# Stick-breaking attention on one core: half a group of weights times values moved to the head of its step

## What is computed

```
def sb_attend(q, q_pos, k, v, k_pos):
    z = jnp.einsum('bqhd,bkhd->bhqk', q, k, preferred_element_type=jnp.float32) * (SB_HEAD_DIM ** -0.5)
    mask = (k_pos[None, :] < q_pos[:, None])[None, None]
    log_keep = jnp.where(mask, jax.nn.log_sigmoid(-z), 0.0)
    suffix = lax.cumsum(log_keep, axis=3, reverse=True) - log_keep
    a = jnp.where(mask, jnp.exp(jax.nn.log_sigmoid(z) + suffix), 0.0)
    return jnp.einsum('bhqk,bkhd->bqhd', a.astype(v.dtype), v)
```

## Time and profile before

| | us |
|---|---|
| median of 3 runs | 2764.31 |
| lowest, highest | 2760.12, 2768.33 |
| the profiled execution | 2768.86 |
| its span, first to last instruction | 2765.2 |
| TensorE busy | 2667.1 (96%) |
| ScalarE busy | 1156.7 (42%) |
| VectorE busy | 1733.0 (63%) |
| GpSimd busy | 732.0 (26%) |

### The profile page before, as it was taken

One profiled execution on the slowest core, in us unless ns is written; L12 is line 12 of the kernel. 1 busy time (PEld: TensorE's weight loads), 2 busy tenths in 40 slices (PEclk: granted clock), 3 DMA queues, 4 the chain that ended last, 5 costly groups with the idle time before them and its releaser, 6 DMA issues. The chain is left out here.

```text
span 2765.2 us, 40402 instructions
## 1 busy us (share of the span) xinstructions
PE 2667.1 (96%) x14531; PEld 2236.8 (81%) x14531; DVE 1733.0 (63%) x2331; ACT 1156.7 (42%) x2260; POOL 732.0 (26%) x627
## 2 busy tenths in 40 slices
PE   7989998999999999999899999998999999999998
PEld 6878887788888878888798887776878888788886
DVE  5656666376555688888410008887485555788887
ACT  4334445343333333344322219998343333333433
POOL 3200001135544400000221116666045544300001
PEclk9999999999999999999999999999999999999999
DMA  4211122514444573533234437763324444654342
GB/s 150 86 61 46 46 79 89 184 60 153 137 137 144 170 256 125 162 122 118 80 128 151 155 102 194 172 173 121 111 95 145 137 137 145 235 181 164 127 154 100
DMA packets 285877, 368.81 MB, mean 133 GB/s; under 512 B 25984, under 2 KB 205696, under 8 KB 285696
## 3 DMA queue, kind: packets, MB, share of 16 engines
q1 hardware_dynamic: 285696, 366.42, 41.7%
HBM read 242.19 MB, written 124.16 MB: 132 GB/s over the span
## 5 line engine op out<-in xcount | busy, mean ns | idle before, releaser
L2342 DVE TENSOR_TENSOR x<-m_ps,x 128x1024 f32<-128x1024 f32 x224 | 273.3, 1220 | 91.9 <-PE m_ps L79 91.8
L2051 POOL TENSOR_TENSOR m_u<-m_u,m_u 128x512 f32<-128x512 f32 x128 | 179.6, 1414 | 349.0 <-DVE m_u L2185 344.0
L1998 POOL TENSOR_SCALAR m_stat<-m_stat 128x1 f32<-128x1 f32 x36 | 12.1, 335 | 831.6 <-ACT m_sqjunk L1942 667.2
L2173 DVE TENSOR_TENSOR m_z<-m_ps,m_part 128x512 f32<-128x512 f32 x96 | 66.3, 691 | 143.8 <-PE m_ps L79 143.5
L1800 ACT COPY m_part<-m_ps 128x512 f32<-128x512 f32 x96 | 56.4, 588 | 205.2 <-PE m_ps L79 205.2
L2161 DVE TENSOR_TENSOR m_up<-m_upr,m_up 128x512 fp32r<-128x512 f32 x128 | 87.9, 707 | 28.5 <-ACT m_up L1787 28.5
L3300 ACT ACTIVATE e_b<-e_ps 128x512 f32<-128x512 f32 (+3 forms) x192 | 95.9, 500 | 12.1 <-PE e_ps L3518 11.6
L1787 ACT CAST m_up<-m_upr 128x512 fp32r<-128x512 f32 x128 | 75.7, 615 | 57.9 <-PE m_ps L79 57.9
L3302 ACT ACTIVATE e_ps<-e_ps 128x512 f32<-128x512 f32 (+3 forms) x192 | 96.3, 501 | 0.0
L2031 POOL TENSOR_TENSOR m_uprS<-m_upr 128x512 f32<-128x512 f32 x62 | 94.6, 1526 | 5.0 <-DVE m_upS3l L2161 4.9
L3583 PE MATMUL e_ps<-ident,e_b 128*128 128x128 f32 x576 | 94.7, 274 | 0.7 <-POOL e_b L3398 0.6
(11 more groups left out here) (1192 smaller groups left out, 9185.8 us busy)
## 6 DMA issues: line engine op xcount, KB each, us to landing
scratch_u<-m_u SPq DMA_DIRECT2D x224, 256.0 KB, 2.1
m_ur<-scratch_u SPq DMA_DIRECT2D x208, 256.0 KB, 2.7
m_upr<-in_mlp_w_up SPq DMA_DIRECT2D x32, 1024.0 KB, 5.9
m_wr<-in_mlp_w_down SPq DMA_DIRECT2D x64, 512.0 KB, 6.6
scratch_x<-x SPq DMA_DIRECT2D x18, 512.0 KB, 2.6
x<-scratch_x SPq DMA_DIRECT2D x8, 1024.0 KB, 9.5
scratch_qr<-a_qrst SPq DMA_DIRECT2D x9, 512.0 KB, 3.4
a_x<-in_x_prompt SPq DMA_DIRECT2D x8, 512.0 KB, 5.0
```

Of the source, the lines that this page charges most:

```text
L2051: pool.tensor_tensor(u_st[out][:], u_st[a][:], u_st[b][:], op).then_inc(u_summed.sem, 1)
L2342: dve.tensor_tensor(out, bank[:, at:at + 2, :], out, ALU.add).then_inc(summed.sem, 1)
```

## The change

Within `step` of TensorE the half of weights times values goes from behind turn 0 to ahead of score piece 0. Only TensorE's list changes, and only in the even steps; no instruction is added or dropped, and each waits for the same as before.

```
             def step(i, n, last, values_of=None):
                 for j in range(3):
+                    if j == 0 and values_of is not None and values_of % 2 == 0:
+                        values(i, values_of // 4, values_of % 4 // 2)
                     if j < len(S.chunks(n + S.AHEAD)) and not (last and n + S.AHEAD >= S.STEPS):
                         scores(i, n + S.AHEAD, j)
                     if j < len(S.tasks(n)) and not (last and n >= S.STEPS):
                         turn(i, n, j)
-                    if j == 0 and values_of is not None and values_of % 2 == 0:
-                        values(i, values_of // 4, values_of % 4 // 2)
```

## The result

The changed kernel takes 2796.8 us, median of 4 runs (2794.0 to 2802.1), against 2764.3 us before in the same comparison: +32.5 us, a ratio of 1.0118 with a 95% interval of 1.0101 to 1.0134. The forecast was 2794 us, +30. The profiled execution took 2802.1 us; its span is 2798.7 us.

The account below looks back on a forecast made before the run. TensorE was taken to set the pace with ScalarE right behind it. Groups 1.0 us longer on average, counted 30 times, gave +30 us on the 2764.3 us median: 2794 us, own range 2785 to 2800 (0.70), 80% range 2778 to 2805.

Parts of the forecast that it names:

- Step one: Start of half 0: it begins 0.05 us after ScalarE's copy ends; ScalarE runs out of work at 0.82 us.
- Step two: Score piece behind half 0's values: ready for ScalarE at 2.01 us, so ScalarE stands for 1.19 us.
- Step three: Stretch to half 1: it starts at 4.21 us, and ScalarE stands for another 0.33 us behind it.
- Step four: Stretch to the next half 0: it starts at 9.19 us instead of 8.07, making the group 1.12 us longer.
- 30 groups, +30 us: Whole stage: 1.0 us more per group, first and last groups not counted, giving +30 us.
- The split: TensorE in the stage: its waits rise from 3.4 to some 26 us; some 8 us come from changed neighbours.
- The costs that no row showed: TensorE: values straight before a score piece, -6 to +6 us; turn before a 32-column task, -3 to 0; both taken as nothing.
- The rule on tiling modes: TensorE's even steps with 32-column sample tasks get one more form change: 32 x 0.18 = 6 us by the rule alone.
- ScalarE did not catch up: Rival at half 0: ScalarE catches up, leaving waits averaging 0.36 us; +16 us, about 2780; chance 0.14.
- Not slower: Rival at half 0: the moved values fill a wait instead of making one; 2761 us; chance 0.07 including little changed.
- A later chain: Rival: VectorE's scans slip behind ScalarE's bursts and score pieces wait for their bank; 2803 us; chance 0.09 with clock.
- The clock: Rival: TensorE's clock falls in the stage, 1.5 us a pair; 2806 us and more; chance 0.09 with a later chain.

Follow-up runs that it names:

- e7: Kernel before plus an extra 128x512 ScalarE copy every fourth step, just behind the copy that half 0 waits for and its signal: 2766.0 us, ratio 1.0005.
- e6: Kernel before plus an extra 128x512 ScalarE copy every fourth step, just ahead of the copy that half 0 waits for: 2775.1 us, ratio 1.0041.
- e4: Changed kernel plus an extra 128x512 ScalarE copy every fourth step, just ahead of the copy that half 0 waits for: 2817.8 us, ratio 1.0177.
- e1: Kernel before with only half 0 of the values moved to the head of its step, half 1 left in place: 2788.5 us, ratio 1.0077.
- e2: Kernel before with only half 1 of the values moved to the head of its step, half 0 left in place: 2773.6 us, ratio 1.0023.
- e9: Changed kernel with turn 0 and its copy ahead of score piece 0 and its sigmoids in steps 4g + 3: 2780.0 us, ratio 1.0049 to before.
- e3: Changed kernel, both halves at the head of a step, but half 0 one step later: 2780.5 us, ratio 1.0049 to before.
- e8: Kernel before with both halves run together behind turn 0 of step 4g + 6: 2773.2 us, ratio 1.0028.
- e5: Changed kernel plus an extra 128x512 ScalarE copy every fourth step, just behind the copy that half 0 waits for and its signal: 2796.4 us, ratio 1.0100.

## Why the prediction was right, point by point

**The frame.** TensorE sets the pace and ScalarE has 1.4 us of 31.8 to spare: held. e7 spent that spare time for 1 us.

**Step one, the copy's 0.05 us and the early end of ScalarE's list.** Held: half 0 starts 0.05 us behind the copy, in all 32 groups TensorE waits for it.

**Step two, 1.19 us of standing.** 1.09 measured in group 8, and 1.20, 0.99 and 0.75 in the three behind it; the prediction had looked for 1.0 to 1.3 in each. The values took 1.24 as before, the piece's mask matmul came 0.46 after its start where I took 0.44, and ScalarE 0.33 after that. The 0.1 us too much is on ScalarE's side: 1.48 us is from start to start, and its last sigmoid ends 0.93 us after the start of half 0 (1741.64 + 0.64 - 1741.35) and not 0.82.

**Step three, half 1 at 4.21 and 0.33 of standing.** 4.23 (1745.58 - 1741.35) and 0.42.

**Step four, 9.19 us for the group.** 9.09. The other seven groups of the two pairs: 9.31, 9.38, 8.63 and 9.27, 8.86, 9.18, 8.69, where the walk had 9.3, 9.4, 8.6 and 9.3, 8.7, 9.2, 8.7. The pairs came out at 36.4 and 36.0 against 36.4 and 35.9.

**30 groups, +30 us.** 31.5 for those 30. The stage as a whole is 35.2 us longer in the profile. The 3.7 that I had no term for are 1.4 at its start and 2.4 at its end; of the latter 1.7 is clock (below). At the start the granted clock was lower than in the earlier trace rows:

```profile
1655.00:1660.00 5.00, 4.88 (x15) 3.37 (x16) 1.97 (x6) 4.18 (x11) 0.42 (x1) 0.50 0.81 271
```

From the first score piece to half 0 of group 0 it is 0.65 here, over 13.8 us, and 0.86 before, over 12.4. Both levels occur with either order, so this is not put down to the change: e6, which has the old order, had 0.67 and 14.3 us in its profile, and e4, which has the new one, 0.87 and 12.9.

**The split.** I had TensorE's wait rise from 3.4 us to some 26, by 22.6, with 8 us for the neighbours. It rose to 24.9, by 21.5, and some 11 are left for the neighbours, a third more than the 8: the two misses cancel in part. That the 11 us belong to the position and not to the wait is shown by the other orders. From half 0 of group 0 to half 0 of group 28, in us:

| | seven pairs | TensorE's waits over 0.15 us | the rest |
|---|---|---|---|
| before | 224.5 | 2.2 | 222.3 |
| changed | 253.7 | 21.8 | 231.9 |
| e1, half 0 alone | 242.8 | 14.9 | 227.9 |
| e2, half 1 alone | 232.1 | 3.8 | 228.3 |
| e9, turn first | 237.2 | 5.0 | 232.2 |
| e3, a step later | 238.2 | 6.8 | 231.4 |
| e8, both in one place | 229.0 | 7.7 | 221.3 |

With both halves at the head of a step the rest is 9 to 10 us longer, whether TensorE waits 22 us or 5; with one half there it is 6 longer, with either.

**The costs that no row showed.** Values straight before a score piece: taken as before a sample task, and it is that (1741.35 to 1742.59 is 1.24 again). The turn before a 32-column task: 0.32 again (1743.12 to 1743.44). Before a 128-column task it is less, 0.23 (1747.12 to 1747.35), as I had it at 0.24. Both costs taken at nothing were right.

**The rule on tiling modes.** The Trainium skill (TensorEngine Tiling (Array Packing), Key Properties) has a change of mode drain TensorE. By that rule, the trace agrees in part. From the last transpose of a turn to a task of 64 or 32 columns it is 0.20 us, start to start, and to a sample task of 128-column transposes 0.11, so 0.09 goes with the change of mode (two transposes: 0.32 us before L3535 above, 0.23 before L3525). But to a score piece, of 128 columns too, it is 0.03. The 0.18 that the prediction read as the price of one change is the distance from 0.03 to 0.20, and only half of it goes with the mode. So an even step whose sample task has 32 columns, with one change more, got 0.17 us longer, and one whose task has 128 columns, with none more, got 0.08 longer. 32 of each make 8 of the 11 us, of which the changes of mode as such are 3 (32 x 0.09); for the other 3 of the 11 I have no reading.

**The rivals.** ScalarE did not catch up: 6.3 us of waits in the pair instead of 1.4. Not slower: the copies came late in every group. A later chain: VectorE is busy for 27 of 36 us, and no matmul and no ScalarE instruction waits for it. The clock: not in the pairs, where it stayed at 1.00, but in the last values of the stage.

## What to carry to other kernels

Work that waits for nothing new can still be a cover: before it is moved ahead, ask which copy was finishing under the pieces that stood in front of it, and whether the engine that makes this copy lives on what comes behind. Where two engines feed each other and both are above 90% busy, carry the rows of both forward through one period; a sum over one engine misses that the wait of the one becomes the idle time of the other. And put every shared buffer into that walk, not only those that bind today: the three banks left out here did no harm to the forecast of the change and are the larger part of why those of e3 and e8 missed.

## What the runs showed of the hardware

The clock of TensorE fell to its lower level behind waits of little more than 1 us, in some places and executions and not in others. In the stage of the kernel before it is 1.00 from 1665 us to the end. In the changed kernel the last values, which start after a wait of 1.24 us, ran partly at 1.2 GHz (first the order of time, then the stretch):

```profile
1947.93 3.85 PE L3599 MATMUL e_ps<-e_pt,e_second_v 128*64 128x256 f32 x20 [1.24 <-ACT e_pt L3327]
```

```profile
1948.00:1952.00 4.00, 4.00 (x34) 2.53 (x36) 2.74 (x2) 1.00 (x2) 2.36 (x1) 0.57 0.00 0
```

In the kernel before the same 20 records took

```profile
1919.37 2.17 PE L3599 MATMUL e_ps<-e_pt,e_second_v 128*64 128x256 f32 x20 [1.19 <-ACT e_pt L3327]
```

behind a wait of 1.19 us, at 1.00. The wait is nearly the same, so its length alone doesn't decide. Nor does the order of work: e5, with the same order on TensorE and the same wait of 1.24 us there, ran these 20 records in 2.17 us at 1.00, and in e4 waits of 1.45 and 1.67 us had a fall behind them in two pairs and none in the other two. What decides is open. The fall cost 1.7 us here (3.85 less 2.17), 1.6 in each of the two pairs of e4 and 1.4 in its last values. With waits of 0.4 to 1.2 us in every 9 the clock stayed at 1.00 through the pairs of the changed kernel.
